# Feed-forward weight slots as eight wide then eight narrow matmuls, with one matmul of each slot cut in two

## What is computed

```python
D_MODEL = 1024; SEQ = 256; DEPTH = 2
D_FF = 256 * ((8 * D_MODEL // 3 + 255) // 256)      # 2816

def swiglu(x, w_gate, w_up, w_down):
    return (jax.nn.silu(x @ w_gate) * (x @ w_up)) @ w_down

for layer in range(DEPTH):
    ...
    h = h + 0.5 * swiglu(rms_norm(h, ffn1_norm_g[layer]), ffn1_w_gate[layer], ffn1_w_up[layer], ffn1_w_down[layer])
    ...
    # layer 0: a convolution and memory attention; layer 1: attention and memory attention
    h = h + jnp.concatenate([primary, mem_out], axis=-1) @ w_o[layer]
    h = h + 0.5 * swiglu(rms_norm(h, ffn2_norm_g[layer]), ffn2_w_gate[layer], ffn2_w_up[layer], ffn2_w_down[layer])
```

## Time and profile before

| | |
|---|---|
| time, median of 3 runs | 1197.43 us (1196.15 to 1197.96) |
| the profiled execution, its own time | 1196.47 us |
| its span, first to last instruction | 1195.2 us |
| PE matmul busy | 1185.7 us (99%), 7514 matmuls |
| DVE / ACT / POOL busy | 872.8 us (73%) / 678.5 us (57%) / 64.9 us (5%) |
| DMA | 215.86 MB, mean 181 GB/s |

### The profile page before, as it was taken

One profiled execution on the slowest core, in us unless ns is written; L12 is line 12 of the kernel. 1 busy time (PEld: TensorE's weight loads), 2 busy tenths in 40 slices (PEclk: granted clock), 3 DMA queues, 4 the chain that ended last, 5 costly groups with the idle time before them and its releaser, 6 DMA issues.

```text
span 1195.2 us, 18861 instructions
## 1 busy us (share of the span) xinstructions
PE 1185.7 (99%) x7514; PEld 1047.3 (88%) x7514; DVE 872.8 (73%) x1243; ACT 678.5 (57%) x1038; POOL 64.9 (5%) x87
## 2 busy tenths in 40 slices
PE   9999999999999999999999999999999999999998
PEld 8888889968888888888888888988888899879996
DVE  7977766876887766777766677687776668666875
ACT  6766654446655545565554457566554545566463
POOL 1501000200010000000000022000000000000000
PEclk9999999999999999999999999999999999999999
DMA  8865656663565555556655553266655565535450
GB/s 303 302 196 178 196 171 203 202 174 124 194 194 190 184 181 188 203 169 209 195 175 179 176 190 126 72 192 191 194 183 178 193 213 178 177 123 192 134 170 36
DMA packets 65399, 215.86 MB, mean 181 GB/s; under 512 B 8352, under 2 KB 12064, under 8 KB 65184
## 3 DMA queue, kind: packets, MB, share of 16 engines
q1 hardware_dynamic: 62608, 210.64, 55.2%
q10 hardware_dynamic: 2704, 4.02, 1.0%
HBM read 212.70 MB, written 1.93 MB: 180 GB/s over the span
## 4 chain that ended last, share of the span: by engine, by line
PE 89%; DVE 4%; ACT 4%; issue 1%; DMA 1%; SPq 0%; POOL 0%; ACTq 0%; POOLq 0%
PE psum L510 88%; DVE wlo L1841 2%; ACT whi L1230 1%; DVE first L2054 1%; DMA raw<-in_slots 1%; PE psum L903 0%; ACT x L1304 0%; ACT sqb L1294 0%; ACT L1680 0%; ACT zob L1680 0%; ACT pb L1725 0%; DVE small L2432 0%; ACT sqb L1665 0%; DVE oa L2492 0%; ACT qn L1549 0%
## 5 line engine op out<-in xcount | busy, mean ns | idle before, releaser
L510 PE MATMUL psum<-x,whi 128*128 128x512 f32 (+1 forms) x2384 | 629.8, 353 | 0.8 <-DVE x L1918 0.3
L1841 DVE TENSOR_TENSOR wlo<-raw,whi 128x1024 fp32r<-128x1024 f32 (+2 forms) x402 | 473.8, 1190 | 165.8 <-ACT whi L1230 162.9
L1230 ACT CAST whi<-raw 128x1024 fp32r<-128x1024 f32 (+2 forms) x402 | 405.2, 1021 | 158.3 <-PE psum L510 153.1
L510 PEld LDWEIGHTS psum<-x,wlo 128*128 128x128 f32 x1960 | 367.9, 188 | 64.9 <-DVE wlo L1841 1.0
L510 PE MATMUL psum<-x,wlo 128*128 128x256 f32 x1960 | 421.7, 279 | 0.5 <-DVE wlo L1841 0.5
L510 PEld LDWEIGHTS psum<-x,whi 128*128 128x128 f32 x2384 | 362.0, 188 | 2.6 <-issue 0.9
L510 PE MATMUL psum<-g,whi 128*128 128x512 f32 x704 | 218.6, 392 | 0.0
L510 PEld LDWEIGHTS psum<-g,wlo 128*128 128x128 f32 x704 | 132.2, 188 | 29.5
L510 PE MATMUL psum<-whi,x 128*128 128x512 f32 (+1 forms) x512 | 140.7, 375 | 0.1
L510 PE MATMUL psum<-g,wlo 128*128 128x256 f32 x704 | 139.1, 279 | 0.0
L510 PEld LDWEIGHTS psum<-g,whi 128*128 128x128 f32 x704 | 106.8, 188 | 0.0
(11 more groups left out here) (315 smaller groups left out, 807.4 us busy)
## 6 DMA issues: line engine op xcount, KB each, us to landing
raw<-in_slots SPq DMA_DIRECT2D x371, 512.0 KB, 4.2
raw<-in_slots SPq DMA_DIRECT2D x16, 384.0 KB, 3.6
raw<-in_slots SPq DMA_DIRECT2D x16, 256.0 KB, 2.9
h<-conv_mem SPq DMA_DIRECT2D x8, 284.0 KB, 5.4
mkv<-in_mem ACTq DMA_DIRECT2D x1, 1024.0 KB, 12.5
memt<-in_mem_cols ACTq DMA_DIRECT2D x1, 1024.0 KB, 15.8
conv_mem<-hc SPq DMA_DIRECT2D x3, 288.0 KB, 3.5
h<-conv_mem SPq DMA_DIRECT2D x4, 142.0 KB, 3.0
```

The costliest lines, as they stand in the source:

```text
L510: return pe.matmul(o, l, r, start=start, stop=stop, skip_group_check=True)
L1230: act.copy(held(B.whi[:, i % SPLIT, :], *n), held(B.raw[:, i % RAW, :], *n)).then_inc(*s.hi.now(i))
L1841: dve.tensor_tensor(held(B.wlo[:, i % SPLIT, :], *n), held(B.raw[:, i % RAW, :], *n), held(B.whi[:, i % SPLIT, :], *n).bitcast(F32), ALU.s ...
```

## The change

In the feed-forward parts (and in the output projections, which share `part`) the order within a slot becomes: all eight wide matmuls, then all eight narrow ones. The wait for `s.lo` moves behind the eighth wide one. Slot 0, which comes in halves, is done as four wide and four narrow, twice.

In each slot of three of the four feed-forward parts one matmul is also cut in two, along its moving columns; both pieces have the same stationary operand and write neighbouring columns of the same bank:

- part 0: nothing is cut;
- part 1 (`"first"`): the first narrow one of the slot, as 128 and 128 columns;
- part 2 (`"last"`): the last narrow one of the slot, as 128 and 128 columns;
- part 3 (`"wide"`): the first wide one of the slot, as 256 and 256 columns.

In the second block, in slots `QK2 + 5` and `AQK2 + 3`, one narrow matmul (third block, first half, high by high) is cut into 128 and 128 columns. In all 206 matmuls are added. The order of instructions on the other engines and of the transfers is the same.

```diff
-    def two_blocks(b, h, l, x, start, stop, ready=None):
+    def rounded(b, h, x, start, cut=False):
         for j in range(2):
-            mm(bank[b + j], h[:, j * 128:(j + 1) * 128], x.rearrange("p a b -> p (a b)"), start, False)
-        if ready is not None:
-            pe.wait_ge(*ready)
+            if cut and j == 0:
+                for e in range(2):
+                    mm(bank[b + j][:, e * S:(e + 1) * S], h[:, j * 128:(j + 1) * 128], x[:, e, :], start and e == 0, False)
+            else:
+                mm(bank[b + j], h[:, j * 128:(j + 1) * 128], x.rearrange("p a b -> p (a b)"), start, False)
+
+    def left(b, l, x, stop, cut=None):
         for j in range(2):
-            t = mm(bank[b + j][:, 0:S], l[:, j * 128:(j + 1) * 128], x[:, 0, :], False, stop)
+            for n in ((0, 128), (128, 256)) if cut == j else ((0, 256),):
+                t = mm(bank[b + j][:, n[0]:n[1]], l[:, j * 128:(j + 1) * 128], x[:, 0, n[0]:n[1]], False, stop)
         return t
...
+        for i in range(0, len(ks), run):
+            if slot:
+                if i == 0:
+                    pe.wait_ge(*s.hi.at(slot))
+            else:
+                pe.wait_ge(*(s.hi.at(0) if i else s.hi0.at("half")))
+            for kc in ks[i:i + run]:
...
+                rounded(b, h[:, kc % 4, :], x[:, kc], start and kc == ks[0], cut == "wide" and kc == ks[0])
+            if slot:
+                if i == 0:
+                    pe.wait_ge(*s.lo.at(slot))
+            else:
+                pe.wait_ge(*(s.lo.at(0) if i else s.lo0.at("half")))
+            for kc in ks[i:i + run]:
+                t = left(b, l[:, kc % 4, :], x[:, kc], stop and kc == ks[-1],
+                         0 if cut == "first" and kc == ks[0] else 1 if cut == "last" and kc == ks[-1] else None)
         t.then_inc(*s.used.now(slot))
...
-                           start and i == 0 and j == 0, stop and kc == ks[-1], slot if i == 0 and j == 0 else None)
+                           start and i == 0 and j == 0, stop and kc == ks[-1], slot if i == 0 and j == 0 else None,
+                           slot in (QK2 + 5, AQK2 + 3) and i == 2 and j == 0)
...
     def ffn(f, x, gen):
         base, F = FFN[f], B.ffn[f]
+        run, cut = 4, (None, "first", "last", "wide")[f]
```

More of the change, by code:

```diff
@@ L538, in two_blocks, with part @@
+    def left(b, l, x, stop, cut=None):
         for j in range(2):
-            t = mm(bank[b + j][:, 0:S], l[:, j * 128:(j + 1) * 128], x[:, 0, :], False, stop)
+            for n in ((0, 128), (128, 256)) if cut == j else ((0, 256),):
+                t = mm(bank[b + j][:, n[0]:n[1]], l[:, j * 128:(j + 1) * 128], x[:, 0, n[0]:n[1]], False, stop)
         return t
-    def part(x, slot, b, ks, start, stop, gen=None, between=None):
+    def part(x, slot, b, ks, start, stop, gen=None, run=4, cut=None):
@@ L544, in part @@
         side(slot)
         h, l = weights(slot, len(ks), 256)
[L547 to L559, removed]
+        ks = list(ks)
@@ L560, in part, with direct @@
         t.then_inc(*s.used.now(slot))
-    def direct(o, h, l, xi, kc, start, stop, ready=None):
-        mm(o, h, xh[xi][:, kc, :], start, False)
+    def direct(o, h, l, xi, kc, start, stop, ready=None, cut=False):
+        for n in ((0, 128), (128, 256)) if cut else ((0, 256),):
+            mm(o[:, n[0]:n[1]], h, xh[xi][:, kc, n[0]:n[1]], start and n[0] == 0, False)
         mm(o, h, xl[xi][:, kc, :], False, False)
@@ L693, in ffn @@
             if p:
-                cols(x, 8, up_slot(f, p), 0)
+                cols(x, 8, up_slot(f, p), 0, None, run, cut)
                 pe.wait_ge(*s.sum.at(("up", f, p - 1)))
-                cols(x, 8, up_slot(f, p) + 2, 2)
+                cols(x, 8, up_slot(f, p) + 2, 2, None, run, cut)
             else:
-                part(x, base, 0, range(4), True, False, gen)
+                part(x, base, 0, range(4), True, False, gen, run, cut)
                 if f in (1, 3):
@@ L702, in ffn @@
                     pe.wait_ge(*s.sum.at(("up", 1, PAIRS - 1)))
-                part(x, base + 1, 2, range(4), True, False)
-                part(x, base + 2, 0, range(4, 8), False, True, gen)
-                part(x, base + 3, 2, range(4, 8), False, True)
+                part(x, base + 1, 2, range(4), True, False, None, run, cut)
+                part(x, base + 2, 0, range(4, 8), False, True, gen, run, cut)
+                part(x, base + 3, 2, range(4, 8), False, True, None, run, cut)
         for p in range(4):
@@ L714, in ffn, with down @@
                 pe.wait_ge(*s.h.at(((1, 3, 4, 6)[f], 0)))
-            down(f, F, down_slot(f, p), (4, 6, 0, 4)[p], p == 0)
-    def down(f, F, slot, b, first):
+            down(f, F, down_slot(f, p), (4, 6, 0, 4)[p], p == 0, run, cut)
+    def down(f, F, slot, b, first, run, cut):
         i = slot
         for k0 in range(0, 22, 4):
-            m = min(4, 22 - k0)
+            ks = list(range(k0, min(22, k0 + 4)))
             side(i)
-            h, l = weights(i, m, 256)
+            h, l = weights(i, len(ks), 256)
             pe.wait_ge(*s.hi.at(i))
[L724 to L729, removed]
+            for r in range(0, len(ks), run):
+                for kc in ks[r:r + run]:
+                    if first and kc % 2 == 0:
+                        pe.wait_ge(*s.g_hi.at((f, kc // 2)))
+                        pe.wait_ge(*s.g_lo.at((f, kc // 2)))
+                    rounded(b, h[:, kc - k0, :], F.g[:, kc], kc == 0, cut == "wide" and kc == k0)
+                if r == 0:
+                    pe.wait_ge(*s.lo.at(i))
+                for kc in ks[r:r + run]:
+                    t = left(b, l[:, kc - k0, :], F.g[:, kc], kc == 21,
+                             0 if cut == "first" and kc == k0 else 1 if cut == "last" and kc == ks[-1] else None)
             t.then_inc(*s.used.now(i))
```

9 lines of the change are left out of this document (7 added, 2 removed).

## The result

| | before | changed |
|---|---|---|
| time, median | 1196.87 us (4 runs, 1196.15 to 1197.96) | 1213.93 us (4 runs, 1212.97 to 1214.61) |
| profiled execution, own time / span | 1196.47 / 1195.2 us | 1214.61 / 1213.4 us |

The changed kernel is slower, by 17.1 us: ratio 1.0141, 95% interval 1.0129 to 1.0153. The forecast was 1211 us, slower by 13.9 us, in a range of 1199 to 1222.

A forecast was written before the change was run, and what follows sets the result against it. PE, busy for 1185.7 of 1195.2 us, was taken as the bound, through distances between matmul starts. The terms -1.0 + 8.5 + 7.8 - 1.1 - 0.5 + 0.2 = +13.9 us took 1197.43 to 1211 us, range 1199 to 1222.

The forecast's parts named there:

- Item 2: Narrow matmuls cut 128 + 128 in parts 1 and 2: +0.105 to +0.110 us per cut, +8.5 and +7.8 us.
- the sign given for it: Parts 1 and 2: starts of two 128-column pieces, with the matmul behind, would span 0.22 us; 0.12 would refute it.
- Item 2, part 2: Cuts in part 2: 44 slots at +0.125 us, 22 down slots at +0.097, half slots 0.2: +7.8 us.
- the surcharge of the earlier trace: Part 2's down slots before the change: 2.79 us each, against 2.76 for a feed-forward slot.
- Items 1 and 3: New order without cuts in part 0, -1.0 us; new order with a wide matmul cut 256 + 256 in part 3, -1.1 us.
- Item 4: The start: wait for wlo gone, slot 3 sooner though chunks of x come late: -0.5 us.
- Item 5: Two narrow cuts in the second block, 0.105 us each: +0.2 us, bounds -1.1 and +0.2.
- nearly free: Rival: second load fetched ahead during wide matmuls, so a cut costs only its columns: about 1193 us, chance 0.11.
- slow throughout: Rival: every run at the slow pace (wide 0.233, narrow 0.118 us): +27.3 us, 1224.7 us, chance 0.10.
- fast throughout: Rival: every run at the fast pace (wide 0.227, narrow 0.113 us): +2.2 us, 1199.6 us, chance 0.14.
- new wait: Rival: chunks of g or x late for eight wide matmuls, 4 us on top: 1215 us, chance 0.03.
- item 3: Part 3, wide matmul cut 256 + 256: pieces cost as two narrow ones, -1.1 us, bounds -2.6 and +3.7.

The follow-up runs named there:

- e1: Changed kernel's order (eight wide, then eight narrow) with no matmul cut anywhere, against the kernel before: 1197.84 us against 1197.39, ratio 1.0003.
- e2: Old order (two wide, two narrow) with all 206 cuts of the changed kernel, against the kernel before: 1216.51 us, ratio 1.0166.
- e4: New order, narrow matmuls cut by part: one 64 + 192, one 192 + 64, two and four 128 + 128; no second-block cuts: 1259.31 us.
- e10: Kernel before with only 48 columns of padding added ahead of g in part 2: 1197.48 us against 1197.34.
- e5: Kernel before with six narrow and six wide matmuls cut in the second block, none in feed-forward parts: 1196.99 us against 1196.25.
- e9: e8 plus padding ahead of g in part 2, old order in slots 100 and 268, more second-block cuts: 1183.97 us against 1197.34.
- e7: Every feed-forward and projection wide matmul from slot 2 cut into 256 + 256, 128-column cuts behind stops: 1206.78 us against 1198.24 before.
- e6: Other orders: part 0 4 + 4 twice, part 2 6 + 6 + 2 + 2, parts 1 and 3 all 256-column matmuls: 1198.93 us against 1196.25 before.
- e8: Old order for a few slots behind each stop, equal 256-column matmuls elsewhere, no 128-column cuts in feed-forward parts: 1189.08 us against 1195.70 before.

## Why the prediction was right, and where its terms were off

The direction, the reason and the range were right: nothing waits, the distances decide, and an added matmul of under 256 columns costs a load. The sum was 3 us short of the measured 17.1. That its errors in parts 1 and 2 (-1.1 and +1.0 us) cancel is luck.

**Item 2, the cuts, held.** It was forecast at 0.105 to 0.110 us a cut and 2.885 us a slot in part 1; the slots took 2.876. e1 and e2 show that the cuts alone carry the loss, e4 that each added matmul costs 0.11 to 0.13 us. The argument under it held too: the load of the second piece starts with the first piece and no sooner. What did not come out is the sign given for it, 0.22 us from the first piece to the matmul behind both: their starts span 0.17 us (403.30 to 403.47), and the next distance carries the rest; it is the loads that lie 0.22 us apart over two. Nor do the cuts put every slot on the slow pace: the seven narrow ones behind a cut go at 0.113 us in one slot of three in part 1. Part 1 came to 1.1 us less than forecast: half by the slot, the other half where slots wait for chunks of `x` anyway and hide the cut (slot 101: 3.130 us before, 2.984 now). By the Trainium skill, page "TensorE: Matmul & The Clock Gate", section "LDWEIGHTS (loading the stationary operand)", a load takes its columns / 1.2 ns, an estimate of 107 ns for 128; e4's 0.112 us for each of four and the 0.11 us between the loads agree. By the section "Back-to-back issue gap" of that page of the Trainium skill a cut would have cost 2.5 ns; e4 speaks against it for pieces shorter than a load.

**Item 2, part 2, was mis-sized (+7.8, measured +8.8).** The step that failed took one duration, 2.885 us, for up and down slots alike, and so let the surcharge of the earlier trace rows go in the down slots. The slots took 2.893 up and 2.916 down. The surcharge stays, because it comes from where `g` lies (e10).

**Items 1 and 3, the order, were mis-sized (-1.0 and -1.1, measured +0.1 and +0.2).** The failing step is "the fast 0.113 us for the narrow ones where nothing disturbs them". The row behind it shows 72 narrow ones in a row; runs of eight between wide ones alternate between the paces (e1). The bounds, 2.72 and 2.81 us, held, and the value is nearly in their middle: 2.757. That a wide cut into 256 + 256 is almost free was right in the new order (+0.007) and not in the old one (+0.033).

**Item 4, the start, held** (-0.5, measured -0.6), with the wait and the chunks of `x` where the forecast put them.

**Item 5 had about the right sum (+0.2, measured 0.0) by another way.** The cut in `QK2 + 5` did not turn the pace, and that in `AQK2 + 3` had nothing to turn. The narrow ones of slot `AQK2` went to the fast pace at the 8-column transposes, ahead of the cut in `AQK2 + 3`:

```profile
1015.38 0.28 PE L510 MATMUL psum<-x,wlo 128*128 128x256 f32 x1
...
1015.73 0.28 PE L510 MATMUL psum<-x,wlo 128*128 128x256 f32 x1
...
1016.29 0.28 PE L1032 MATMUL psum<-ident,oa 8*128 8x8 f32 x2
...
1017.18 0.28 PE L510 MATMUL psum<-x,wlo 128*128 128x256 f32 x1
...
1017.52 0.28 PE L510 MATMUL psum<-x,wlo 128*128 128x256 f32 x1
```

Three take 0.35 us ahead of them and 0.34 behind. That gave 0.6 us back in slots 343 to 350, with the cost of one cut in it, after 0.4 lost in slots 334 to 342, and 0.2 were lost further on. e1, which has neither cut, gained 0.7 us in slots 343 to 350, so the cuts didn't do it. The new order alone is no sure way to it either: e4, with the new order and other cuts in the feed-forward parts, took 23.03 us there as before. What decides at the transposes stays open.

**Missed altogether:** the pace of what follows a feed-forward part. The 72 narrow ones of the earlier trace rows, slots 72 to 74, are at 0.118 us in the changed kernel (+0.3 us), and they are so in e1 too, so the new order of part 0 is enough for it (in e4, with cuts in part 0 besides, they stay at 0.113 us); slots 234 to 265 lost another 0.3. In the traces the rest of the gap is the clock dip of the changed kernel's profile; between the medians it has no part.

One bound was added up wrong: item 3 at the slow pace is 66 x 0.051 = +3.4 us, not +3.7, and the slow rival 0.3 us less. Neither carries the forecast.

Of the rivals, "nearly free" fell by e4, "slow throughout" and "fast throughout" by the alternation, and no new wait came.

What stays open is what sets the pace. e5 to e9 show how it can be turned and that it lasts, and e7 that a recipe for one place fails in another. No run tells what in PE keeps the rhythm.

## What to carry to other kernels

Where PE is busy all the time, price an edit in distances between starts, and never cut a matmul below the length of its weight load: every piece costs a load (0.111 us here). Long runs of equal matmuls settle into one of two paces, 3 to 4% apart; look at the distances behind each stop, and let a slow run be entered from another pattern. Splitting 512 into 256 + 256 was nearly free in runs of eight wide ones (+0.007 us), less so between pairs (+0.033), and makes all matmuls of a slot equal.

## What the runs showed of the hardware

- Equal matmuls over 256 columns go steadily at 0.1133 or 0.1178 us for hundreds in a row (slots of 24: 2.720 or 2.827 us; e6 to e9), and wide ones at 0.227 or 0.233. A single added matmul of 128 columns can turn the first kind (e5), and six wide ones cut into 256 + 256 did not turn the second.
- Where the moving operand lies in SBUF changes PE's pace: 192 bytes of shift in each partition took slots from 2.787 to 2.760 us (e10) and, in runs of equal matmuls, from 2.848 to 2.720, 4.5% (e8, e9).
- The load for the second piece of a cut matmul starts together with the first piece, even behind eight wide matmuls, and the next loads follow 0.11 us apart (changed kernel, 403.30 to 403.52 us). The second piece itself starts 0.06 us behind the first, and the matmul behind the pieces is the one that is followed late, by 0.17 in place of 0.11 us.
- The granted clock fell to its lower level for some 3.3 us at about 275 us, behind 24 matmuls over 4 columns, in the profiles of the changed kernel and of e10 (0.89 in the stretch 271 to 286 us) and not in that of before (1.00), though e10 gives PE the same matmuls as before. It costs 1.6 us by the slots, and 1.5 us lie between the two groups of times of the kernel before.
